# Gate products inside a U tile, one PSUM layout for both layers, and gathers of U rows ordered anew

## The reference

```
q = (ht @ w_q).reshape(t, PEER_HEADS, 2, PEER_HALF)
sc = jnp.einsum('thid,hikd->thik', q, keys)
top_s, top_i = lax.top_k(sc, PEER_TOPK)
cand = top_s[:, :, 0, :, None] + top_s[:, :, 1, None, :]
best_s, best_pos = lax.top_k(cand.reshape(t, PEER_HEADS, PEER_TOPK * PEER_TOPK), PEER_TOPK)
i1 = jnp.take_along_axis(top_i[:, :, 0], best_pos // PEER_TOPK, axis=-1)
i2 = jnp.take_along_axis(top_i[:, :, 1], best_pos % PEER_TOPK, axis=-1)
experts = i1 * N_KEYS + i2
gates = jax.nn.softmax(best_s, axis=-1)
...
act = jnp.einsum('thkd,td->thk', u_tab[eb], hb)
coef = gb * jax.nn.gelu(act, approximate=False)
return jnp.einsum('thk,thkd->td', coef, v_tab[eb])
```

## Time and profile before

| | us |
|---|---|
| median of 3 runs | 2918.89 |
| lowest and highest of them | 2910.59, 2923.99 |
| the profiled execution | 2918.5 |
| its span | 2916.8 |

### The profile page before, as it was taken

The page is one execution under the profiler, slowest core; times in us unless marked ns, Lnnn a source line. Parts: engine busy times, 40 slices in busy tenths (PEclk is TensorE's granted clock), DMA queues, the critical chain, the costliest instruction groups (busy, mean ns, idle before and its releaser), DMA issues.

```text
span 2916.8 us, 49290 instructions
## 1 busy us (share of the span) xinstructions
PE 2856.3 (98%) x17864; PEld 2649.9 (91%) x17864; DVE 2490.2 (85%) x5020; ACT 1370.6 (47%) x2321; POOL 951.8 (33%) x773
## 2 busy tenths in 40 slices
PE   7999999999999999999999999999999999999998
PEld 4777789999999999999988788999999999999998
DVE  4667788998989899999986789889888879999998
ACT  3344234477766333333353532446666643333333
POOL 1000028633334334434300001773333343434442
PEclk9999999999999999999999999999999999999999
DMA  7425648899999999999921122789999899999996
GB/s 281 170 108 194 248 147 288 309 360 381 389 365 340 349 376 387 385 386 376 371 87 59 65 79 94 252 285 333 371 359 370 308 341 347 384 382 383 379 383 253
DMA packets 252535, 855.05 MB, mean 293 GB/s; under 512 B 25568, under 2 KB 58592, under 8 KB 245728
## 3 DMA queue, kind: packets, MB, share of 16 engines
q1 hardware_dynamic: 149280, 442.23, 41.4%
q0 software_dynamic: 98496, 381.73, 35.1%
q10 hardware_dynamic: 4608, 29.36, 2.5%
HBM read 777.06 MB, written 76.15 MB: 293 GB/s over the span
## 4 chain that ended last, share of the span: by engine, by line
PE 85%; DVE 6%; DMA 4%; ACT 2%; issue 2%; SPq 0%; POOL 0%; DVEq 0%; ACTq 0%; POOLq 0%
PE banks L1085 42%; PE banks L1620 31%; PE banks L1581 4%; PE banks L1418 2%; DMA w_raw<-wst 2%; DVE w_lo L1661 1%; PE banks L1155 1%; DMA activations<-act_out 1%; PE banks L1505 1%; ACT w_hi L799 1%; DMA pj<-adaw 1%; DVE ring L2161 1%; PE banks L1101 1%; DVE h L1679 1%; DVE vacc L2173 0%
## 5 line engine op out<-in xcount | busy, mean ns | idle before, releaser
L799 ACT ACTIVATE w_hi<-w_raw 128x1024 fp32r<-128x1024 f32 x596 | 630.5, 1058 | 825.2 <-PE banks L1085 692.5
L1085 PE MATMUL banks<-hH,w_hi 128*128 128x352 f32 (+1 forms) x2528 | 878.7, 348 | 14.0 <-ACT act_out L1012 6.1
L1661 DVE TENSOR_TENSOR w_lo<-w_raw,w_hi 128x1024 fp32r<-128x1024 f32 x522 | 638.5, 1223 | 283.9 <-ACT w_hi L799 281.5
L1085 PE MATMUL banks<-hL,w_hi 128*128 128x352 f32 (+1 forms) x2528 | 854.3, 338 | 0.0
L1085 PE MATMUL banks<-hH,w_lo 128*128 128x352 f32 (+1 forms) x2528 | 854.1, 338 | 0.0
L763 POOL DMA_INDIRECT ring<-v,gidx x320 | 398.1, 1244 | 602.5 <-DVE vacc L2173 526.6
L1085 PEld LDWEIGHTS banks<-hH,w_hi 128*128 128x128 f32 x2528 | 481.2, 190 | 62.6 <-issue 24.2
L1085 PEld LDWEIGHTS banks<-hH,w_lo 128*128 128x128 f32 x2528 | 477.3, 189 | 19.5
L1085 PEld LDWEIGHTS banks<-hL,w_hi 128*128 128x128 f32 x2528 | 478.4, 189 | 17.3 <-issue 0.5
L1620 PE MATMUL banks<-c_lo_late,w_hi 128*128 128x352 f32 x1536 | 494.0, 322 | 0.0
L763 POOL DMA_INDIRECT ring<-u,gidx x260 | 291.3, 1121 | 517.4 <-DVE gact L2161 506.4
(11 more groups left out here) (354 smaller groups left out, 3977.4 us busy)
## 6 DMA issues: line engine op xcount, KB each, us to landing
w_raw<-wst SPq DMA_DIRECT2D x596, 512.0 KB, 6.4
activations<-act_out SPq DMA_DIRECT2D x124, 352.0 KB, 7.0
act_in<-activations SPq DMA_DIRECT2D x62, 704.0 KB, 7.9
gate_matrices<-stages ACTq DMA_DIRECT2D x32, 896.0 KB, 9.6
gates<-gate_matrices SPq DMA_DIRECT2D x64, 448.0 KB, 10.2
ada_buf<-adaw POOLq DMA_DIRECT2D x24, 1024.0 KB, 7.1
nrm<-adaw POOLq DMA_DIRECT2D x8, 1024.0 KB, 5.2
pj<-adaw POOLq DMA_DIRECT2D x7, 1024.0 KB, 7.1
```

Of the source, the lines that this page charges most:

```text
L799: nc.scalar.activation(w_hi[g % 2][:, :, :].rearrange("p a b -> p (a b)"), w_raw[:, g % RAWS, :], ACT.Copy).then_inc(s_wh, 1)
L1085: last = mm(bank[s][:, 0:t.stop - t.start], a[s][:, k, :], b[:, k, t], start=(k == 0 and a is w_hi and b is hH), stop=(k == KT - 1 and a i ...
L1661: v.tensor_tensor(w_lo[g % 2][:, :, :].rearrange("p a b -> p (a b)"), w_raw[:, g % RAWS, :], w_hi[g % 2][:, :, :].rearrange("p a b -> p (a ...
```

## The change

1. **Gate products.** `project` gets an argument `halfway`; in the gate stage `gate_quad` and its three waits are called after 12 of the tile's 24 matmuls. They stood behind the 24. ACT's and DVE's lists are as before there.
2. **Layout.** `by_expert` is that of layer 0 in both layers.
3. **Stores.** STORES goes from 4 to 8: 64 stores of 448 KB in place of 32 of 896 KB.
4. **Gathers.** AHEAD goes from 30 to 38. POOL issues its gathers after the `lo` of tiles 10 to 38, one at each and two where n % 3 is 1 (39 in place of 26). DVE does 4, 11 and 14 early `gather_u` steps in blocks 1, 2 and 3 (before: 6, 7, 7); the 4 of block 1 come behind both `picked` steps. In tiles 37 to 41 it does 9 (before 10), one of them at tile 37 (before 2). The rest is spread by rates over tiles 42 to 124.

```
-STORES = 4
+STORES = 8
...
-EARLY_GATHERS = (0, 6, 7, 7)
-EARLY = sum(EARLY_GATHERS)
-AHEAD = 30
+EARLY_GATHERS = ((0, 0, 0, 0), (0, 0, 0, 4), (0, 3, 3, 5), (3, 4, 4, 3))
+EARLY = sum(sum(early) for early in EARLY_GATHERS)
+AHEAD = 38
...
-POOL_GATHER_AT = [11, 12, 13, 14, 15, 16, 17, 18, 19, 20, 21, 22, 23, 24, 25, 26, 27, 28, 29, 30, 31, 33, 34, 35, 37, 38]
+POOL_GATHERS = [0] * N_KEYS
+for _n in range(10, GATHER0 + 2):
+    POOL_GATHERS[_n] = 2 if _n % 3 == 1 else 1
 U_GATHERS = [0] * N_KEYS
 for _n in range(GATHER0, GATE0):
-    U_GATHERS[_n] = 2
+    U_GATHERS[_n] = 2 if _n > GATHER0 else 1
...
+GATHER_RATES = ((GATE0, 55, 170), (55, 105, 138), (105, GATE1, 173), (GATE1, N_KEYS - 3, 100))
...
-        def by_expert(l, q):
+        def by_expert(q):
-            return bank[2 + q % 2][:, :].rearrange("p (t e) -> p e t" if l == 0 else "p (e t) -> p e t", t=QUAD)
+            return bank[2 + q % 2][:, :].rearrange("p (t e) -> p e t", t=QUAD)
...
                 for k in range(KT):
+                    if k == KT // 2 and halfway is not None:
+                        halfway()
                     for a, b in ((w_hi, hH), (w_hi, hL), (w_lo, hH)):
...
+                def gates_of(n, i=0):
+                    for u in quads_of(n):
+                        pe.wait_ge(s_oh, l * QUADS + u + 1 + i * per)
+                        pe.wait_ge(s_bp, l * QUADS + u + 1 + i * per)
+                        pe.wait_ge(s_gv, l * QUADS + u + 1 + i * per)
                         gate_quad(u)
...
-                for n in range(GATE0 + loops * GATE_LOOP, GATE1):
-                    u_tile(n, n % 2)
+                for n in range(GATE0 + GATE_LOOPS * GATE_LOOP, GATE1):
+                    u_tile(n, n % 2, lambda: gates_of(n))
...
                 for tt in range(NT):
                     first_rows(tt)
                     candidates(tt)
+                    early_gathers(EARLY_GATHERS[tt][0])
                     best_pairs()
...
                     for a in range(2):
-                        for _ in range(early // 3):
-                            gather_u(gathered)
-                            gathered += 1
+                        early_gathers(EARLY_GATHERS[tt][1 + a])
                         picked(tt, a)
```

More of the change, by code:

```diff
@@ L157 @@
 AHEAD_SET = 4
-POOL_GATHER_AT = [11, 12, 13, 14, 15, 16, 17, 18, 19, 20, 21, 22, 23, 24, 25, 26, 27, 28, 29, 30, 31, 33, 34, 35, 37, 38]
+POOL_GATHERS = [0] * N_KEYS
+for _n in range(10, GATHER0 + 2):
+    POOL_GATHERS[_n] = 2 if _n % 3 == 1 else 1
 U_GATHERS = [0] * N_KEYS
 for _n in range(GATHER0, GATE0):
-    U_GATHERS[_n] = 2
[L162 to L166, removed]
+    U_GATHERS[_n] = 2 if _n > GATHER0 else 1
+assert EARLY + sum(U_GATHERS) == AHEAD and sum(POOL_GATHERS) <= AHEAD + RING
+GATHER_RATES = ((GATE0, 55, 170), (55, 105, 138), (105, GATE1, 173), (GATE1, N_KEYS - 3, 100))
+_due = 0
+for _first, _last, _rate in GATHER_RATES:
+    for _n in range(_first, _last):
+        _due += _rate
+        U_GATHERS[_n] = min(1 if len(quads_of(_n + 1)) > 1 else 2, _due // 100)
+        _due -= U_GATHERS[_n] * 100
 assert sum(U_GATHERS) + EARLY == UG and U_GATHERS[N_KEYS - 1] == 0, (UG - EARLY, sum(U_GATHERS))
@@ L772, in _ @@
                         load_ada(1, c)
+                k = 0
                 for n in range(POOL_LO0, POOL_LO1):
@@ L776, in _ @@
                     lo(l, n)
-                    if n - U0 == POOL_GATHER_AT[0]:
+                    if n - U0 == POOL_GATHERS.index(max(POOL_GATHERS)):
                         if l == 0:
@@ L780, in _ @@
                         pool.wait_ge(s_gidx, l + 1)
-                    if n - U0 in POOL_GATHER_AT:
-                        gather(l, POOL_GATHER_AT.index(n - U0))
-                for k in range(len(POOL_GATHER_AT), GATHERS):
+                    for _ in range(POOL_GATHERS[n - U0]):
+                        gather(l, k)
+                        k += 1
+                for k in range(sum(POOL_GATHERS), GATHERS):
                     gather(l, k)
@@ L1040, in _ @@
                         nc.scalar.activation(
-                            home[:, :, i * QUAD:(i + 1) * QUAD], by_expert(l, q),
+                            home[:, :, i * QUAD:(i + 1) * QUAD], by_expert(q),
                             ACT.Copy, scale=2.0 ** -GATE_UP).then_inc(s_gv, 1)
@@ L1073, in _, with project @@
             steps = Steps(pe, None, s_pset)
-            def project(l, n, s, tokens=None):
+            def project(l, n, s, tokens=None, halfway=None):
                 t = slice(0, T) if tokens is None else tokens
@@ L1519, in _, with u_tile @@
                             modulation(1, 0, 4)
-                def u_tile(n, s):
-                    project(l, U0 + n, s, tokens=slice(TG, T))
+                def u_tile(n, s, halfway=None):
+                    project(l, U0 + n, s, tokens=slice(TG, T), halfway=halfway)
                 def route_rows(tt):
@@ L1580, in gate_quad @@
                         for part in range(2):
-                            last = mm(by_expert(l, u)[:, :, t], oh[:, 2 + part, t, :], oh[:, 1, t, :].bitcast(BF16),
+                            last = mm(by_expert(u)[:, :, t], oh[:, 2 + part, t, :], oh[:, 1, t, :].bitcast(BF16),
                                       start=(part == 0), stop=(part == 1))
                     last.then_inc(s_gm, 1)
[L1585 to L1597, removed]
-                for n in range(GATE0 + loops * GATE_LOOP, GATE1):
-                    u_tile(n, n % 2)
+                def gates_of(n, i=0):
                     for u in quads_of(n):
-                        pe.wait_ge(s_oh, l * QUADS + u + 1)
-                        pe.wait_ge(s_bp, l * QUADS + u + 1)
-                        pe.wait_ge(s_gv, l * QUADS + u + 1)
+                        pe.wait_ge(s_oh, l * QUADS + u + 1 + i * per)
+                        pe.wait_ge(s_bp, l * QUADS + u + 1 + i * per)
+                        pe.wait_ge(s_gv, l * QUADS + u + 1 + i * per)
                         gate_quad(u)
+                with pe.Fori(0, GATE_LOOPS) as i:
+                    for j in range(GATE_LOOP):
+                        u_tile(i * GATE_LOOP + (GATE0 + j), j % 2, lambda: gates_of(GATE0 + j, i))
+                for n in range(GATE0 + GATE_LOOPS * GATE_LOOP, GATE1):
+                    u_tile(n, n % 2, lambda: gates_of(n))
                 with pe.Fori(GATE1 // 2, N_KEYS // 2) as i:
@@ L2327, in _, with early_gathers @@
                 gathered = 0
+                def early_gathers(count):
+                    nonlocal gathered
+                    for _ in range(count):
+                        gather_u(gathered)
+                        gathered += 1
                 for tt in range(NT):
@@ L2333, in _ @@
                     decoded()
-                    early = EARLY_GATHERS[tt]
                     if tt == 1:
@@ L2337, in _ @@
                     for a in range(2):
-                        for _ in range(early // 3):
-                            gather_u(gathered)
-                            gathered += 1
+                        early_gathers(EARLY_GATHERS[tt][1 + a])
                         picked(tt, a)
-                    for _ in range(early - 2 * (early // 3)):
-                        gather_u(gathered)
-                        gathered += 1
+                    early_gathers(EARLY_GATHERS[tt][3])
                     gated(tt)
```

## The result

The changed kernel takes 3129.83 us (median of 4 runs, 3125.02 to 3133.18) against 2919.2: a ratio of 1.0724, 95% interval 1.0694 to 1.0754. The forecast was 3140.

What follows compares the result with a forecast made beforehand. PE's matmuls, busy 98% of the time, were taken to bound the kernel. 2918.5 + 200.4 (gate stage) + 9 (gathers, net) + 12 (clock) = 3140 us; range 3096 to 3210.

Steps and rivals of the forecast that it cites:

- The ring: Gate stage: PE's products await ACT's scalings, which await the previous tile's end; 5.85 us a tile, +200.4 us together.
- The 112.0 and 86.9 of the sum: Microseconds added from first to last gate products in layer 0 and layer 1, each reaching 469 us.
- The clock: Gate stage: PE's stops at tiles with two quads and the next lower the granted clock; +12 us, bounds 0 to 68.
- The rival in which it swings all the time: Gate stage: stops in every tile keep the clock low for part of each; 125 us more, 3265; chance 0.09.
- The gathers on POOL: Tiles before the gate stage: paired gathers delay w_lo, PE waits 0.8 us at ten tiles a layer; 15 us taken.
- The stores: Gate stage: 32 more store issues by ACT taken at nothing, or 16 us if their cover were gone.
- The layout: Layer 1's products fall from 0.80 to 0.42 us, 33.4 us in all, already in the 5.85 us a tile.
- The rival "in time": Gate stage: ACT's scalings ready within 2.08 us of a tile's end, so nothing stops; 2902 us, chance 0.06.

Runs made afterwards that it cites:

- place6: The changed kernel with the gate products behind 18 of the tile's 24 matmuls instead of 12: 2967.7 us, ratio 1.0171 to the kernel before.
- place2: The changed kernel with the gate products behind 6 of the tile's 24 matmuls instead of 12: 3309.9 us, ratio 1.1371 to the kernel before.
- stores_alone: The kernel before with 8 store parts a chunk in place of 4, nothing else: 2903.8 us, ratio 0.9962.
- gathers_alone: The kernel before with the changed kernel's gather settings, nothing else: 2910.5 us, ratio 0.9985.
- mid_alone: The kernel before with the gate products moved to the middle of the tile, nothing else: 3153.3 us, ratio 1.0809.
- behind: The changed kernel with the gate products put back behind the tile's 24 matmuls: 2869.6 us, ratio 0.9839 to the kernel before.

## Why the prediction was right, point by point

**The ring.** 5.85 us a tile were computed; 5.81 were read. For a tile with two quads 1.66 more were computed, and 1.17 + 6.30 - 5.81 = 1.66 were read (the tile at 718.64). 469 us of stage were computed; with 5.81 the same sum is 466, and the clock's 6 and 7 us (below) make up most of what the 473.9 and 474.8 are above it. place6, at a granted clock of 1.00, comes within 0.1 of its own computed number, though a little by offsetting: its tile is 4.87 against 4.89, its stores cost more than the 2 counted. The 112.0 and 86.9 of the sum are 117 and about 92 in the trace, clock included (473.9 - 357.0, 474.8 less 382.1 and the 0.7 between the first and last of eight matmuls).

**The clock.** Taken at 12 in all, seven falls, 0 to 68 as bounds. The granted clock over the two stages is 0.99 and 0.98, and tile by tile it fell nine times. In layer 0 it fell behind four of the ten pairs of quads, in layer 1 behind two, for about 1.5 us each. In layer 1 it also fell behind three stops of 1.87 us at a chunk's first store, for 1.0 to 1.4 each. That is 6 and 7 us. The other pairs had the same two stops and kept the clock, and no run tells why; seven was a guess with no working behind it, and that it came close is luck. It fell in such tiles as that at 670.05, whose second stop can be seen above, and the stretch of the changed kernel behind it has:

```profile
669.50:673.10 3.60, 3.05 (x16) 3.08 (x17) 2.11 (x5) 0.45 (x2) 1.99 (x2) 0.60 0.84 281
```

The rival in which it swings all the time did not come at 1.34 us of stop. place2, with 2.30 us in every tile, shows the start of it, and still only 4 to 5% of the clock. The Trainium skill's section cited beside that rival (TensorE: Matmul & The Clock Gate, "A second HAM failure mode: psum-queue depth-cycling") tells of a clock that swings with short stops between groups of matmuls. The traces agree in kind only: nine falls in 156 tiles of the changed kernel and 31 in place2, not one in every tile.

**The gathers on POOL.** A pair of gathers puts two w_lo 4.80 apart, it was said. In the changed kernel, POOL in order of time and PE's stop at such a tile:

```profile
437.54 2.40 POOL L755 TENSOR_TENSOR w_lo<-w_raw,w_hi 128x1024 fp32r<-128x1024 f32 x1 [1.64 <-ACT w_hi L806]
442.35 2.40 POOL L755 TENSOR_TENSOR w_lo<-w_raw,w_hi 128x1024 fp32r<-128x1024 f32 x1
450.20 2.41 POOL L755 TENSOR_TENSOR w_lo<-w_raw,w_hi 128x1024 fp32r<-128x1024 f32 x1 [0.81 <-ACT w_hi L806]
...
444.85 0.40 PE L1094 MATMUL banks<-hH,w_hi 128*128 128x352 f32 x1 [0.77 <-issue]
```

They are 4.81 apart and PE stands 0.77. But three tiles take 450.20 - 437.54 = 12.66, against 3 x 4.01: 0.63 net, since the two tiles behind make a part up. At ten places that is 6 a layer, not 8: 12 in all, where 15 were taken.

**What was left out: the end of the stage.** Before, PE stood once more, ahead of the last tiles:

```profile
959.61 1.06 ACT L799 ACTIVATE w_hi<-w_raw 128x1024 fp32r<-128x1024 f32 x1 [7.08 <-DMA w_raw<-wst]
...
962.32 0.40 PE L1085 MATMUL banks<-hH,w_hi 128*128 128x352 f32 x1 [3.37 <-ACT act_out L1012]
```

PE's waits of the kernel before have 6.1 us for it in two places, those of stores_alone still 5.5, those of gathers_alone and of the changed kernel none. So it is the gathers that take it away, and at least 6 us were left out of the sum (in both places the clock is low for 11 matmuls behind the stop). (Their rates leave fewer for the tiles behind the gate stage; that this is the way was not tried by itself.) This and 3 us less for POOL are most of what 3140 is too high by, 10 above the median and 15 above the profiled execution's 3125.0. Against that execution, the two stages grew by 208.9 us where 198.9 + 12 were forecast, and everything outside them shrank by 2.4 where it was to grow by 10.5: 13 of the 15 us lie outside. The first products' waits for DVE's one-hots, 1.22 and 1.52 us, were left out too, with the other sign: DVE is not in the ring, but it sets its start.

**The stores.** The issues cost about what was counted (0.54 us at a chunk's first part, 6.35 against 5.81). But for the eight parts as a whole "taken at nothing, or a cost of 16" was the wrong side: on the kernel before they gain 10 us. That this did no harm to the forecast is luck: at a DMA share of 0.83 the ring has no use for it. mid_alone, with the four long stores, has the same stage in layer 0 (473.1). The bounds looked at ACT's time of issue and not at who shares the DMA engines, though the stage was read as held by DMA at 0.97.

**The layout.** It is in the ring as counted: mid_alone, without it, has 24 us more in layer 1 (of 77 x 0.38 = 29). Alone it gives 28, where 26 were expected.

**The rival "in time"** put 2902 for a kernel whose scalings come early enough. With the products behind the tile nothing waits for the scalings either, and that kernel (behind) takes 2870: wrong by the stores (about 10 a layer, as both layers now run at the same rate) and by the stop at the end of the stage.

## What to carry to other kernels

When a step is moved forward in one engine's list, count for each thing it reads what stands ahead of it in the maker's list, and from which event that list starts; here ACT had been idle for some 30% of the stage and yet set its time. Where a consumer releases the maker and the maker the consumer, the time of a round is the sum of both parts, and only what lies inside it is worth moving. A stage that is held by DMA can gain from the size of its stores alone: here 11 us of 357 came at a DMA share of 0.97 from half as long stores of the same bytes. Whether it carries over to another kernel is not shown.

## What was not expected of the hardware

- Stores of 448 KB in place of 896 KB, same bytes, took the waits for w_raw and for the stores of activations out of layer 0's gate stage (13.5 and 9.1 us of ACT), and 10 us off the time, although the median load took 7.4 us to land in place of 6.9.
- PE may stop for 1.34 us in every 5.8 and keep its granted clock at 0.98 to 0.99; at stops of 2.30 us in every 6.8 it is still 0.95 to 0.96, as the clock falls in 14 and 17 of 78 tiles only. A stop of 1.34 and one of 0.56 right behind it brought it down in 6 of 20 places.
- A tile's chain of matmuls was broken for products into another bank at no cost that shows: behind 21 of 24, two usual tiles take 8.90 us against 8.84 with the products behind them, and behind 18 of 24 the stage is 395.0 and 394.9 us where the sum of its parts is 395.
